# Scores of two attention branches from stacked halves: single-pass matmuls in place of float32 ones, on one core of a Trainium2

## What is computed

```python
scores = jnp.einsum('bhncd,bhnsd->bhncs', qf, kf) * decay[None, :, None]   # retention, rotary q and k
z = jnp.einsum('bhqd,bhkd->bhqk', q_blk, kf) * scale                       # stick-breaking, no rotary
```

## Time and profile before

| | us |
|---|---|
| median of 3 runs | 1311.41 (1311.26 to 1311.43) |
| the profiled execution's own time | 1311.28 |
| its span in the trace | 1309.4 |
| PE busy in it | 1286.9 (98%) |
| DVE busy | 863.1 (66%) |
| ACT busy | 643.6 (49%) |
| POOL busy | 39.8 (3%) |

### The profile page before, as it was taken

How to read it: one execution, slowest core, us unless ns; L and a number is a source line. 1 busy time by engine, 2 the same in 40 slices (tenths; PEclk the granted TensorE clock), 3 DMA queues, 4 the chain that set the end, 5 groups by cost and what they waited for, 6 DMA issues and landing times.

```text
span 1309.4 us, 26212 instructions
## 1 busy us (share of the span) xinstructions
PE 1286.9 (98%) x10294; PEld 1278.3 (98%) x10294; DVE 863.1 (66%) x1076; ACT 643.6 (49%) x830; POOL 39.8 (3%) x37
## 2 busy tenths in 40 slices
PE   6999999999999999999999999999999999999996
PEld 6999999999999999999999999999999999999996
DVE  7666556757776776665566665577667767766654
ACT  4444445545656554444444444455456565544431
POOL 1000000000000010000000000000000001000000
PEclk9999999999999999999999999999999999999999
DMA  7655554654434556565556555546544445666561
GB/s 257 198 172 174 178 177 151 190 166 138 129 118 141 165 163 187 177 176 177 177 161 181 174 176 177 176 148 196 172 133 126 141 155 172 195 188 184 175 199 56
DMA packets 61205, 219.13 MB, mean 167 GB/s; under 512 B 6992, under 2 KB 8144, under 8 KB 61008
## 3 DMA queue, kind: packets, MB, share of 16 engines
q1 hardware_dynamic: 60704, 217.53, 54.3%
q10 hardware_dynamic: 432, 0.59, 0.2%
HBM read 217.04 MB, written 1.05 MB: 167 GB/s over the span
## 4 chain that ended last, share of the span: by engine, by line
PE 96%; DVE 2%; ACT 1%; DMA 1%; issue 0%; DVEq 0%; SPq 0%; ACTq 0%
PE bank L867 30%; PE bank L868 30%; PE bank L866 30%; PE bank L1093 1%; PE bank L1065 1%; PE bank L1048 1%; PE bank L1080 1%; PE bank L961 1%; DMA raw<-stream 1%; DVE w_lo L524 0%; PE bank L944 0%; PE bank L968 0%; PE bank L880 0%; PE bank L881 0%; PE bank L1055 0%
## 5 line engine op out<-in xcount | busy, mean ns | idle before, releaser
L524 DVE TENSOR_TENSOR w_lo<-raw,w_hi 128x1024 fp32r<-128x1024 f32 x408 | 509.1, 1252 | 283.3 <-ACT w_hi L343 277.5
L866 PE MATMUL bank<-xh,w_hi 128*128 128x272 f32 (+1 forms) x2240 | 645.1, 288 | 11.6 <-DVE xl L538 11.1
L343 ACT ACTIVATE w_hi<-raw 128x1024 fp32r<-128x1024 f32 x408 | 428.0, 1056 | 437.9 <-PE bank L868 434.1
L867 PE MATMUL bank<-xl,w_hi 128*128 128x272 f32 (+1 forms) x2240 | 642.4, 287 | 0.0
L868 PE MATMUL bank<-xh,w_lo 128*128 128x272 f32 (+1 forms) x2240 | 640.5, 286 | 0.0
L866 PEld LDWEIGHTS bank<-xh,w_hi 128*128 128x128 f32 x2240 | 423.5, 189 | 12.6 <-DVE xl L538 10.1
L867 PEld LDWEIGHTS bank<-xl,w_hi 128*128 128x128 f32 x2240 | 422.0, 188 | 0.2
L868 PEld LDWEIGHTS bank<-xh,w_lo 128*128 128x128 f32 x2240 | 421.9, 188 | 0.0
L866 PE MATMUL bank<-gh,w_hi 128*128 128x272 f32 (+1 forms) x1024 | 292.9, 286 | 0.0
L867 PE MATMUL bank<-gl,w_hi 128*128 128x272 f32 (+1 forms) x1024 | 292.1, 285 | 0.0
L868 PE MATMUL bank<-gh,w_lo 128*128 128x272 f32 (+1 forms) x1024 | 291.9, 285 | 0.0
(11 more groups left out here) (159 smaller groups left out, 635.9 us busy)
## 6 DMA issues: line engine op xcount, KB each, us to landing
raw<-stream SPq DMA_DIRECT2D x408, 512.0 KB, 3.6
table<-tables SPq DMA_DIRECT2D x1, 1424.0 KB, 8.7
out<-h SPq DMA_DIRECT2D x4, 256.0 KB, 2.4
h<-tokens ACTq DMA_DIRECT2D x2, 272.0 KB, 5.7
h<-tokens SPq DMA_DIRECT2D x2, 272.0 KB, 6.0
rv_gb<-squares SPq DMA_DIRECT2D x1, 384.0 KB, 8.4
square<-squares SPq DMA_DIRECT2D x1, 128.0 KB, 7.9
gain<-gains ACTq DMA_DIRECT2D x1, 28.0 KB, 4.7
```

The costliest lines, as they stand in the source:

```text
L343: eng.activation(w_hi[:, slot, :], raw[:, slot, :], ACT.Copy).then_inc(hi_ready, 1)
L524: eng.tensor_tensor(w_lo[:, slot, :], raw[:, slot, :], w_hi[:, slot, :].bitcast(F32), ALU.subtract).then_inc(lo_ready, 1)
L866: pe.matmul(out, wh, hi, start=first, stop=False)
L867: pe.matmul(out, wh, lo, start=False, stop=False)
```

## The change

Queries and keys of both branches are split as the weights are. `qs` holds for each head the rounded queries in the head's own 64 rows and their remainders in the other 64. Each head has a chunk of `gh` and of `gl`, buffers that are free at that time: in `gh` the rounded keys lie in the head's own rows and the remainders in the other 64, in `gl` the two are swapped. A head's scores are then, for each of the two tiles, one F32R matmul with the chunk of `gh` and one with that of `gl`, which together give all four products. Matmuls of L1065 and L1093 become `scores`: four F32R ones for a head instead of two float32 ones. What fills the stacks, for each layer:

- ACT: at step 11 the rounded retention queries (2 instructions of 64x1088), at 34 and 40 the stick-breaking ones (2 of 64x544 each); for each branch at 12 and 14, or 27 and 29, the rounded keys into `gh` (2 of 64x512 each time), one step later the same into `gl`, and at 16 and 17, or 31 and 32, a copy of the remainders from `gl` to `gh`.
- DVE: the remainders of the queries behind the split of steps 12 (2 of 64x1088), 35 and 41 (2 of 64x544 each). The rotary queries (one instruction for two) go to `sk`, the stick-breaking ones (one for L739's two or three) to `rk`.
- POOL: the remainders of the keys (`keys_lo`, 4 of 64x512 for each branch), the queries of the last 16 tokens (`place_tail_queries`); the copies of L321 are gone.

```diff
@@ -74,6 +74,8 @@
 ADDS = PAIRS - 1
 RET0, SB0 = 24, 37
 RET_TAIL, SB_TAIL = 20, 36
+Q_HI = [11, 34, 40]
+K_HI = [12, 27]
 NEG = -2.0 ** 100
 
 
...
@@ -101,14 +103,14 @@
-        qz = sb("qz", [P, 4, 2, T])
+        qs = sb("qs", [P, 4, 2, T], F32R)
...
-        sq1 = sb("sq1", [P, 2, T])
-        sqz_tail = sb("sqz_tail", [P, 2, 2, TAIL])
+        rqz_tail = sb("rqz_tail", [P, 4, 2, TAIL])
+        sqz_tail = sb("sqz_tail", [P, 4, 2, TAIL])
...
@@ -181,9 +183,22 @@
+        def stack_chunk(branch, hd):
+
+            return RET_C + hd if branch == 0 else SB_C + hd if hd < 4 else MERGE_C + hd - 2
+
+        def stacks(g, branch, unit, rows, parity):
+
+            c0 = stack_chunk(branch, 4 * unit)
+            return g[rows:rows + DK, c0:c0 + 4, 0:TAIL0].rearrange("p (c i) t -> p c i t", i=2)[:, :, parity, :]
...
@@ -307,18 +323,37 @@
+            def place_tail_queries(dst, queries, placed):
+
+                pool.wait_ge(pads_ready, 3)
+                for i, f0 in enumerate((0, DK)):
+                    mm = pool.tensor_copy(dst[f0:f0 + DK, :, i, :], all_pairs(queries)[f0:f0 + DK, :, TAIL0:T])
+                mm.then_inc(placed, 1)
+
+            def keys_lo(l, branch, keys):
+
+                for unit in range(2):
+                    pool.wait_ge(k_hi, l * 8 + 4 * branch + 2 * (unit + 1))
+                    for i, f0 in enumerate((0, DK)):
+                        pool.tensor_tensor(stacks(gl, branch, unit, f0, i), keys_of(keys, unit, f0),
+                                           stacks(gh, branch, unit, f0, i).bitcast(F32), ALU.subtract).then_inc(k_lo, 1)
+
...
                 place_keys(rk)
+                pool.wait_ge(key_tail_ready, 2 * l + 1)
+                place_tail_queries(rqz_tail, sk, rq_tail_in)
+                keys_lo(l, 0, rk)
+                pool.wait_ge(k_lo, l * 8 + 4)
...
                 place_keys(sk)
+                pool.wait_ge(key_tail_ready, 2 * l + 2)
+                keys_lo(l, 1, sk)
                 pool.wait_ge(unit_evicted, evicted(l, U_SQ[1]))
-                pool.wait_ge(ret_scores, l * HEADS + HEADS)
-                for i, f0 in enumerate((0, DK)):
-                    pool.tensor_copy(qz[f0:f0 + DK, 2:4, i, qf:T], sq1[f0:f0 + DK, :, qf:T]).then_inc(sq1_placed, 1)
+                place_tail_queries(sqz_tail, rk, sq_tail_in)
+                pool.wait_ge(sq_tail_in, l + 1)
...
@@ -496,6 +538,32 @@
+                    if s == Q_HI[0]:
+                        eng.wait_ge(rotated, l * U_V + U_K)
+                        queries_hi(sk, 0, 4)
+                    for unit in range(2):
+                        for branch, keys in ((0, rk), (1, sk)):
+                            if s == K_HI[branch] + 2 * unit:
+                                if branch == 0:
+                                    eng.wait_ge(rotated, l * U_V + U_K + unit + 1)
+                                else:
+                                    eng.wait_ge(unit_evicted, evicted(l, U_SK + unit))
+                                for i, f0 in enumerate((0, DK)):
+                                    eng.activation(stacks(gh, branch, unit, f0, i), keys_of(keys, unit, f0), ACT.Copy).then_inc(k_hi, 1)
+                            if s == K_HI[branch] + 2 * unit + 1:
+                                for i, f0 in enumerate((0, DK)):
+                                    eng.activation(stacks(gl, branch, unit, DK - f0, i), keys_of(keys, unit, f0),
+                                                   ACT.Copy).then_inc(k_stacked, 1)
+                            if s == K_HI[branch] + 4 + unit:
+                                eng.wait_ge(k_lo, l * 8 + 4 * branch + 2 * (unit + 1))
+                                for i, f0 in enumerate((0, DK)):
+                                    eng.activation(stacks(gh, branch, unit, DK - f0, i), stacks(gl, branch, unit, f0, i).bitcast(F32),
+                                                   ACT.Copy).then_inc(k_stacked, 1)
+                        if s == Q_HI[1 + unit]:
+                            eng.wait_ge(unit_evicted, evicted(l, U_SQ[unit]))
+                            eng.wait_ge(ret_scores, l * HEADS + 4 * (unit + 1))
+                            queries_hi(rk, 2 * unit, 2)
...
@@ -621,14 +689,8 @@
-                        if k < U_K:
-                            eng.wait_ge(pads_ready, 2)
-                            c = 2 * k
-                            eng.tensor_tensor(qz[0:DK, c:c + 2, 0, q0:T], uk[0:DK, :, q0:T], tk[0:DK, :, q0:T], ALU.add)
-                            eng.tensor_tensor(qz[DK:P, c:c + 2, 1, q0:T], uk[DK:P, :, q0:T], tk[DK:P, :, q0:T],
-                                              ALU.add).then_inc(rotated, 1)
-                        else:
-                            eng.tensor_tensor(pair_of(rk, 2 * (k - U_K)), uk, tk, ALU.add).then_inc(rotated, 1)
+                        dst = pair_of(sk if k < U_K else rk, 2 * (k % U_K))
+                        eng.tensor_tensor(dst[:, :, q0:T], uk[:, :, q0:T], tk[:, :, q0:T], ALU.add).then_inc(rotated, 1)
...
@@ -734,23 +796,14 @@
                             if u == U_SQ[0]:
-                                eng.wait_ge(ret_scores, l * HEADS + 4)
-                                for i, f0 in enumerate((0, DK)):
-                                    mm = scaled_queries(qz[f0:f0 + DK, 0:2, i, q0:T], slice(f0, f0 + DK), slice(q0, T))
-                            else:
-                                eng.wait_ge(pads_ready, 4)
-                                for i, f0 in enumerate((0, DK)):
-                                    scaled_queries(sqz_tail[f0:f0 + DK, :, i, :], slice(f0, f0 + DK), slice(TAIL0, T))
-                                mm = scaled_queries(sq1[:, :, q0:T], slice(0, P), slice(q0, T))
-                            mm.then_inc(unit_evicted, 1)
+                                eng.wait_ge(k_stacked, l * 16 + 8)
+                                eng.wait_ge(key_tail_ready, 2 * l + 1)
+                            eng.scalar_tensor_tensor(pair_of(rk, 2 * U_SQ.index(u))[:, :, q0:T], res, DK ** -0.5, rb,
+                                                     ALU.mult, ALU.mult).then_inc(unit_evicted, 1)
                         elif u < U_SV:
+                            if u == U_SK:
+                                eng.wait_ge(rq_tail_in, l + 1)
                             eng.tensor_tensor(pair_of(sk, 2 * (u - U_SK)), res, rb, ALU.mult).then_inc(unit_evicted, 1)
...
@@ -790,6 +843,13 @@
+                    for part, queries, c, n in ((0, sk, 0, 4), (1, rk, 0, 2), (2, rk, 2, 2)):
+                        if s == Q_HI[part] + 1:
+                            eng.wait_ge(q_hi, l * 6 + 2 * (part + 1))
+                            for i, f0 in enumerate((0, DK)):
+                                eng.tensor_tensor(qs[DK - f0:2 * DK - f0, c:c + n, i, qf:T], all_pairs(queries)[f0:f0 + DK, c:c + n, qf:T],
+                                                  qs[f0:f0 + DK, c:c + n, i, qf:T].bitcast(F32), ALU.subtract).then_inc(q_ready, 1)
...
@@ -962,11 +1022,22 @@
+                def scores(b, branch, hd):
+
+                    chunk = stack_chunk(branch, hd)
+                    for i, (t0, _) in enumerate(TILES):
+                        q = max(t0, qf)
+                        c = SEG[i] + q - t0
+                        for g in (gh, gl):
+                            mm = pe.matmul(bank[:, b, c:c + T - q], g[:, chunk, t0:t0 + P], qs[:, hd // 2, hd % 2, q:T],
+                                           start=(i == 0 and g is gh), stop=True, skip_group_check=True)
+                    return mm
...
@@ -1059,12 +1130,9 @@
-                        for i, (t0, _) in enumerate(TILES):
-                            q = max(t0, qf)
-                            c = SEG[i] + q - t0
-                            mm = pe.matmul(bank[:, 4, c:c + T - q], key_tile(rk, hd, t0),
-                                           qz[:, hd // 2, hd % 2, q:T], start=(i == 0), stop=True, skip_group_check=True)
-                        mm.then_inc(ret_scores, 1)
+                            pe.wait_ge(k_stacked, l * 16 + 8)
+                            pe.wait_ge(q_ready, l * 6 + 2)
+                        scores(4, 0, hd).then_inc(ret_scores, 1)
...
@@ -1085,24 +1153,21 @@
-                        if hd == 4:
-                            pe.wait_ge(sq1_placed, 2 * l + 2)
-                        for i, (t0, _) in enumerate(TILES):
-                            q = max(t0, qf)
-                            c = SEG[i] + q - t0
-                            pe.matmul(bank[:, 6, c:c + T - q], key_tile(sk, hd, t0),
-                                      qz[:, hd // 2, hd % 2, q:T], start=(i == 0), stop=True, skip_group_check=True)
-
+                        if hd == 0:
+                            pe.wait_ge(k_stacked, l * 16 + 16)
+                        if hd % 4 == 0:
+                            pe.wait_ge(q_ready, l * 6 + 4 + hd // 2)
+                        scores(6, 1, hd)
...
```

(27 more changed lines are left out.)

9 lines of the change are left out of this document (2 added, 7 removed).

## The result

| | before | after |
|---|---|---|
| median | 1311.38 us (1311.26 to 1311.43, 5 runs) | 1317.35 us (1317.30 to 1319.09, 5 runs) |
| the profiled execution | 1311.28, span 1309.4 | 1317.30, span 1315.5 |

A forecast was written before the change was run, and what follows sets the result against it. PE, busy for 1286.9 of 1309.4 us, was taken as the bound. New waits of 9.8 us, less 0.5 that goes and 7.3 saved, gave +2.0 on 1311.28: forecast 1313.4, own range 1311.5 to 1315.5, widest 1308.6 to 1317.5.

The forecast's parts named there:

- no change that can be told: The verdict forecast for the whole kernel: a time within about 0.2%, 1308.8 to 1314.0 us, on the slow side; 47%.
- score blocks: PE's four F32R matmuls per block, narrow ones at 0.11 us each, save 0.24 or 0.22 a block, 7.3 us in all.
- waits that go (step 34): PE no longer waits at step 34 for DVE's queries, now one instruction: 0.5 us gained for both mixers.
- step 12, seen at step 14: DVE's query and POOL's key remainders alternate at a shared port, POOL first; PE waits 3.1 us in each mixer.
- steps 27 to 29: POOL's key remainders delay DVE's split and the decay behind it; PE waits about 0.4 us in each mixer.
- steps 35, 36: DVE's two remainders, 1.28 us together, push L652 back; PE waits 0.8 us in each mixer.
- steps 41 to 43: The same 1.28 us of DVE remainders delay L674's end; PE waits 0.6 us in each mixer.
- Rival 1: DVE goes first at the port at step 12, saving 1.28 us a mixer: 1310.8 us; 15%.
- rival 2: DVE and POOL don't collide; step 12 costs 0.6 us and step 29 nothing: 1307.6 us; 13%.
- rival 4: DVE's backlog reaches step 16, costing 0.6 us more at step 14 and about 0.6 there, each mixer: 1315.8; 12%.
- The clock row should stay at its level: A sign to check in the changed kernel's profile: PE's granted clock stays at the upper level, costing nothing.
- rival 3: PE's clock falls in the new 3.1 us gap for one piece, costing 2.3 us in each mixer: 1318.0 us; 13%.

The follow-up runs named there:

- experiment 6: Changed kernel with retention queries split at steps 18 and 19, stick-breaking remainders as one 128-row instruction instead of two of 64 (wrong results, timing only): 1304.44 us.
- experiment 1: Two runs on the changed kernel: retention query split moved to steps 18 and 19, 1308.95 us; instead, retention key split moved to steps 16 to 21, 1310.29 us.
- experiment 2: Changed kernel with DVE's stick-breaking query remainders at steps 36 and 42 instead of 35 and 41: 1313.3 us.
- experiment 3: Changed kernel with retention queries split at steps 18 and 19 and stick-breaking remainders at steps 36 and 42: 1304.31 us.
- experiment 4: As experiment 3, but each stick-breaking remainder made in two halves, at steps 36 and 38, and 42 and 44: 1303.87 us.
- experiment 7: Changed kernel without the work that fills the stacks and without PE's waits for it (wrong scores): 1302.76 us.

## Why the prediction was off

The time lies 4.0 us above the forecast, inside the widest range (to 1317.5) but above the forecast's own (to 1315.5), and "no change that can be told" was wrong. Two steps of the prediction failed. Its sum put the clock at nothing, and that measured 3.0 us. It priced two remainders of 544 columns at 1.28 us, by rows of instructions on all 128 rows, and the four waits behind them came out 2.0 us longer. An error the other way, 0.8 us at steps 27 to 29, hid part of this. Term by term, for both mixers:

| term | predicted | measured |
|---|---|---|
| score blocks | -7.3 | -7.35 |
| waits that go (step 34) | -0.5 | -0.67 |
| step 12, seen at step 14 | +6.2 | +3.12 + 2.87 = +6.0 |
| steps 27 to 29 | +0.8 | 0 |
| steps 35, 36 | +1.6 | +1.19 + 1.31 = +2.5 |
| steps 41 to 43 | +1.2 | +1.06 + 1.24 = +2.3 |
| clock | 0 | 2 x 1.5 = +3.0 |
| first matmul behind each of the six waits | 0 | 6 x 0.1 = +0.6 |
| sum | +2.0 | +6.4 |

In the traces the first mixer is 3.17 us longer and the second 3.23, which is 6.4 together. The profiled executions differ by only 6.0, since 0.3 us is saved behind the last piece, in every kernel with the change, and 0.06 ahead of the mixers.

**What PE saves: right.** Wide matmuls cost 0.125 and the first narrow one 0.07 (303.61 to 303.68), the second 0.11 (303.68 to 303.79). The new block is 0.43 instead of 0.47. That the first matmul behind it costs 0.17 instead of 0.125 takes 0.04 of it back. The choice of 0.11 for both was wrong in its reason, and right in its sum by luck.

**Step 12: right, and shown.** Order at the port, its alternation and its size came as laid out, and the two moves take it apart: away with the meeting, 4.1 us; away with DVE's instructions, 6.0. The rule of the Trainium skill that the prediction named (SBUF — State Buffer, Who interferes with whom) agrees with this at 64 rows too, 2.33 and 2.29 us against 1.30 alone. Rival 1 (DVE first) and rival 2 (no collision) are out, and so is rival 4: PE does not wait at step 16.

**Steps 27 to 29: the order at the port.** The prediction let POOL's instruction take the port ahead of the split. In the trace the split was there first:

```profile
311.91 1.23 DVE L592 TENSOR_TENSOR w_lo<-raw,w_hi 128x1024 fp32r<-128x1024 f32 x1 [1.57 <-ACT w_hi L378]
310.58 3.71 POOL L338 TENSOR_TENSOR gl<-sk,gh 64x512 fp32r<-64x512 f32 x2 [2.02 <-ACT gh L552]
```

The split takes its usual 1.23 and POOL's second instruction stretches. 0.8 us fell away. POOL's first instruction takes 1.37 (3.71 less the 2.34 of the second) and is done at 311.95, so the split, ready at 311.91, had its turn before the second. By the prediction's own figures POOL's second instruction would have come 0.20 us ahead of the split (307.8 + 1.28 = 309.08 against 309.28), and it came 0.04 behind it. A lead that small decided a term of 0.8 us, and the prediction gave the order no rival here.

**Steps 36 and 43: the failed size.** The wait was foreseen, by 0.8 and 0.6 against 1.19 to 1.31 and 1.06 to 1.24. "On that line 544 columns cost 0.64" was taken from instructions of 128 rows that follow each other, each starting about 0.08 before the former's end. On alternating halves of the rows there is no such overlap, and experiment 6 shows the 0.12 for each of three borders. That is 0.34 of the 0.39 to 0.64 missing at each place. At step 36 of the first mixer the way from L714's end (342.41) to PE's start (342.47) makes up the rest. In the second mixer PE had less in hand than in the first, whose rows alone the prediction used. These are the rows of the second, before:

```profile
987.63 0.42 DVE L652 TENSOR_TENSOR gl<-gv,gh 128x256 fp32r<-128x256 f32 x1
988.35 0.28 PE L1055 MATMUL bank<-gh,square_r 128*128 128x256 f32 x1
```

L652 ends 0.30 us ahead of PE there, and 0.48 in the earlier trace rows. Together the two terms were 2.0 us too small. A rule that would have pointed at this was there and was not weighed: by the Trainium skill, VectorE: DVE Perf Modes, section Two Vector instructions with no wait between them, an instruction is held until every earlier DVE instruction has finished, if an input of it starts in another group of 32 rows than the first input of the last one, or its output in another than the last output (inputs and outputs in the same memory). Here L851 reads rows 0 to 63 and writes rows 64 to 127, the second the other way round, and L708 starts at row 0 again: three held instructions, and three starts 0.03 us behind the end of the one before. The trace agrees.

**The clock: the failed chance.** "The clock row should stay at its level" was wrong, and rival 3 had 13%. What it got right is that a wait costs more than its length; the size was 1.5 us instead of 2.3, since the stretch is 3.4 us at 0.10 for each matmul and not a whole piece. What it got wrong is the place: behind the 2.96 us in the first mixer nothing fell, and the fall of that mixer came behind step 36, where PE had waited 1.03 us. So it is luck that its 1318.0 lies near the measured 1317.35. It should have been weighed for all six new gaps, and not for the two long ones alone. The rule of the Trainium skill (TensorE: Matmul & The Clock Gate, Part 1), that an idle engine drops to half its clock until it is busy again, has the trace's agreement in the drop and its size: 0.50. But PE is busy for the whole 3.4 us at the lower clock, and 2.96 us of idling once had no fall behind it. The Trainium skill says in the same part that the unit which gates the clock watches activity in windows that run freely and don't start with the kernel, and so the place of a transition varies from run to run. The runs of experiments 1 and 2, which lie 1.4 to 1.5 us apart in steps, fit that; no run here shows the windows themselves.

**What stays open** is which gap has a fall behind it. At step 14 of the kernel before, gaps up to 1.6 us had none in 19 runs and gaps from 3.1 us had them in 8 of 8, by their times and mean clocks. In the changed kernel and its relatives a gap of 2.96 us had none and one of 2.9 us in experiment 2 had one; behind a gap of 1.03 us at step 36 there was one, and in the profiled run of experiment 1 the gap there, of 1.11 us, had none. Nor does a stretch begin at a fixed distance from the gap: in these traces it began from 2.3 us before PE started again (the longest gap, second mixer) to 2.1 us after (step 36). The steps of 1.5 us between runs of one kernel say that it differs from execution to execution, as do the two runs of the changed kernel at 1318.85 and 1319.09, whose mean granted clock is 0.994 against 0.995 and 0.996 in the three at 1317.3: one more stretch would give that, but they have no trace. What else has to come together (at step 36 the gap stands beside score blocks and small matmuls, at step 14 beside pieces alone) no run here tells apart. That a gap is what lets the clock fall is shown for those of 3.1 us and more, which were put into the kernel before. For the shorter ones it is argued: the kernels without a gap over 0.3 us (the one before, and those of experiments 3, 4, 6 and 7) show no steps of 1.5 us between their runs.

## What to carry to other kernels

A saving on the engine that bounds the kernel survives only as far as its new helpers find room on the others: here 7.35 us of PE time were turned into a loss of 6.0 by helpers that stood in front of something PE wanted within 2 us, and two edits of their step numbers gave 13 us back. Before placing such work, list for each step how early the semaphore behind it comes, and keep two-input instructions of DVE and POOL out of each other's time. Count 1.5 us on top of a new gap of PE as a possible price (sure here at 3.1 us and more, seen behind one of 1.0, absent in 8 runs with 1.6), and look for it in windows of a few us, since forty slices don't show it.

## What was unexpected of the hardware

- DVE instructions that read or write the other 64 rows than the one before them start 0.03 us after its end, where instructions on the same 128 rows start 0.08 before it. Two of 64x544 take 1.50 us start to start, one of 128x544 takes 0.63.
- A wait of PE can be followed by 3.4 us at a granted clock of 0.50, with PE busy throughout, at a cost of 1.5 us. A wait of 4.6 us once had 6.9 us at that clock, which began inside the gap.
- An F32R matmul of 144 columns behind one of 272 has the next start 0.07 us later; a second one behind it 0.11. Behind a wait of PE, the first matmul of 272 columns has the next start 0.23 us later and not 0.125, at the upper clock.
